# The odd layer's output projection between the attention's units, and four modulation runs elsewhere, in a two-model block kernel

## The reference, cut to what matters

```
cond = silu(c)
mod = cond @ ada_w[l] + ada_b[l]                 # 1024 -> 6 * 1024, both layers
sh1, sc1, g1, sh2, sc2, g2 = split(mod, 6)
h = rms_norm(x, norm_mix[l]) * (1 + sc1) + sh1
q, k, v = split(h @ w_in_odd)                    # 16 heads of 64, 4 key heads
q, k = rms_norm per head
y = banded attention with a sink per head, window 128, softmax over two blocks of 128 keys
x = x + g1 * (y @ w_out[l])
h = rms_norm(x, norm_ffn[l]) * (1 + sc2) + sh2
x = x + g2 * ((silu(h @ gate) * (h @ up)) @ down)
```

## Time and profile before

| | |
|---|---|
| median of three runs | 1477.8 us |
| the profiled execution: its time, its span | 1480.7 us, 1478.7 us |
| mean granted TensorE clock | 0.864 of full |
| PE busy | 1207.3 us, 82% |
| DVE busy | 615.7 us, 42% |
| ACT busy | 476.1 us, 32% |
| chain that ended last | PE 61%, DMA 21%, DVE 9%, ACT 5% |
| 16 DMA engines, main queue | 64.7% of the span |

### The profile page before, as it was taken

The page is one execution under the profiler, slowest core; times in us unless marked ns, Lnnn a source line. Parts: engine busy times, 40 slices in busy tenths (PEclk is TensorE's granted clock), DMA queues, the critical chain, the costliest instruction groups (busy, mean ns, idle before and its releaser), DMA issues.

```text
span 1478.7 us, 19441 instructions
## 1 busy us (share of the span) xinstructions
PE 1207.3 (82%) x7691; PEld 883.7 (60%) x7691; DVE 615.7 (42%) x1239; ACT 476.1 (32%) x769; POOL 7.6 (1%) x54
## 2 busy tenths in 40 slices
PE   5878886775676756847897888999999978999998
PEld 4655464442333323413675337899898734999986
DVE  3472643110010000101753576655535756565553
ACT  4561530100000000002532335554433447465441
POOL 1000000000000000000000000000000000000000
PEclk9897788888888877977897668899999988999999
DMA  8442347999999999999536431865536462665520
GB/s 292 172 152 76 115 173 320 428 430 429 430 430 428 430 430 428 430 425 403 197 129 228 171 114 58 253 207 201 195 145 226 171 253 90 203 196 174 203 109 29
DMA packets 121728, 368.67 MB, mean 249 GB/s; under 512 B 9842, under 2 KB 56093, under 8 KB 110878
## 3 DMA queue, kind: packets, MB, share of 16 engines
q1 hardware_dynamic: 120556, 367.26, 64.7%
q10 hardware_dynamic: 1074, 0.08, 0.1%
HBM read 366.28 MB, written 1.05 MB: 248 GB/s over the span
## 4 chain that ended last, share of the span: by engine, by line
PE 61%; DMA 21%; DVE 9%; ACT 5%; issue 3%; SPq 1%; DVEq 0%; ACTq 0%
PE ps L1810 58%; DMA more<-in_w_down_dram 7%; DMA more<-in_w_gate_dram 7%; DMA more<-in_w_up_dram 6%; PE ps L1814 3%; DVE st L32 2%; DVE ring_r L32 2%; DVE R_c L32 1%; SPq L664 1%; DVE R_a L32 1%; DVE X_c L32 1%; ACT X_c L32 1%; DVE sc L32 1%; ACT R_a L32 1%; ACT hn L32 1%
## 5 line engine op out<-in xcount | busy, mean ns | idle before, releaser
L1810 PE MATMUL ps<-hT_r,ring_r 128*128 128x256 f32 x864 | 245.5, 284 | 0.0
L1810 PE MATMUL ps<-ring,xg 128*32 128x512 f32 x640 | 140.4, 725 | 121.5 <-DMA more<-in_w_gate_dram 42.6
L1810 PEld LDWEIGHTS ps<-hT_r,ring_r 128*128 128x128 f32 x864 | 167.8, 194 | 0.0
L1810 PEld LDWEIGHTS ps<-ring,xg 128*32 128x32 f32 x640 | 35.2, 131 | 217.2 <-issue 217.2
L32 DVE TENSOR_TENSOR ring_r<-ring,W_c_r 128x1024 fp32r<-128x1024 f32 x94 | 115.2, 1226 | 97.5 <-ACT W_c_r L32 94.1
L1810 PE MATMUL ps<-R_c_r,W_c_r 128*128 128x256 f32 x608 | 153.1, 284 | 0.0
L32 DVE TENSOR_TENSOR ring_r<-ring,X_c_r 128x1024 fp32r<-128x1024 f32 x88 | 107.8, 1225 | 98.4 <-ACT X_c_r L32 95.7
L1810 PE MATMUL ps<-R_c_r,X_c_r 128*128 128x256 f32 x576 | 148.2, 285 | 0.0
L32 ACT ACTIVATE W_c_r<-ring 128x1024 fp32r<-128x1024 f32 x94 | 99.7, 1060 | 89.2 <-PE ps L1810 84.5
L32 ACT ACTIVATE X_c_r<-ring 128x1024 fp32r<-128x1024 f32 x88 | 93.3, 1061 | 90.3 <-PE ps L1810 85.4
L1810 PE MATMUL ps<-hT_r,W_c_r 128*128 128x256 f32 x416 | 119.0, 286 | 1.9 <-DVE R_c_r L32 1.8
(11 more groups left out here) (281 smaller groups left out, 1874.5 us busy)
## 6 DMA issues: line engine op xcount, KB each, us to landing
ring<-in_ada_w_dram SPq DMA_DIRECT2D x24, 2048.0 KB, 8.2
ring<-in_w_gate_dram SPq DMA_DIRECT2D x20, 2048.0 KB, 15.9
ring<-in_w_up_dram SPq DMA_DIRECT2D x20, 2048.0 KB, 20.7
ring<-in_w_down_dram SPq DMA_DIRECT2D x20, 2048.0 KB, 16.4
more<-in_w_up_dram SPq DMA_DIRECT2D x12, 2048.0 KB, 24.4
more<-in_w_gate_dram SPq DMA_DIRECT2D x12, 2048.0 KB, 23.1
more<-in_w_down_dram SPq DMA_DIRECT2D x12, 2048.0 KB, 23.6
ring<-in_ffn_gate_dram SPq DMA_DIRECT2D x22, 1024.0 KB, 5.6
```

Of the source, the lines that this page charges most:

```text
L1810: return pe.matmul(out, lhsT, rhs, start=start, stop=stop, skip_group_check=True)
```

## The change

The odd layer's attention and its output projection become one loop, `beside`. `pipeline` is split into a generator `ticks` and `run`, so that one tick can be taken at a time. In tick t = 4 + 2c every engine feeds chunk c of w_out, and PE uses it four ticks later, at t = 8, 10, ..., 18 for chunks 0 to 5; chunks 6 and 7 follow together after the last tick. PE waits for `s_fin` of unit 2c + 1 before chunk c.

To make room in PSUM the scores use banks 0 and 1 for every unit, the turned weights bank 2, and the projection sums banks 3, 4, 5 and 7. All eight chunks of w_out use three of the six high-part buffers (`narrow`).

The seven runs in the attention become three, at units 1, 3 and 5. Run 17 goes to q1's first chunk, run 18 to q1's fourth, runs 22 and 23 to chunks 6 and 12 of the odd layer's down product. The two loads of w_out move in SP's order from after run 21's to after run 19's.

```diff
+def beside(g, units, feed, i0, lag):
+    for t in range(units + 5):
+        next(g, None)
+        k = t - lag + 3
+        if t == lag - 1:
+            feed.side.end()
+        if k >= 0 and k % 2 == 0 and k < 16:
+            feed(i0 + k // 2)
+        elif k == 16:
+            feed.one()
+    feed.drain()
...
     p.product("q0", 4)
-    p.product("q1", 4)
-    p.units(4, 16, (0, 2, 4, 6, 8, 10, 12), 8, 2)
-    p.close(("o", 2))
+    p.ada(("f", len(p.chunks)))
+    k = p.load("w", "q1")
+    p.first["q1"] = len(p.chunks)
+    for q in range(4):
+        if q == 2:
+            p.close(("f", len(p.chunks)))
+        if q == 3:
+            p.ada(("f", len(p.chunks)))
+        p.feed(k, q)
+    p.units(4, 16, (1, 3, 5), 1, 2)
     p.out_proj(2)
-    p.ffn(1, False, None)
+    p.ffn(1, False, (6, 12))
...
-        beside = {first["wo", j] + c for j in range(3) for c in range(2)}
+        narrow = {first["wo", j] + c for j in range(3) for c in range(8 if j == 2 else 2)}
...
+        banks = [(0, 0, 1, 1, 2, 2, 3, 4), (0, 0, 1, 1, 2, 2, 3, 4), (3, 3, 4, 4, 5, 5, 7, 7)]
...
+        t4.score, t4.turned = lambda U, m: m, lambda U: 2
...
                 def used(i):
                     c = i - first["wo", j]
                     if c == 0:
-                        take(0, 1, 2, 3, 4)
+                        take(*(set(banks[j and 2 * j - 2]) if j else range(4)))
+                    if j == 2:
+                        pe.wait_ge(s_fin, t4.fin[2 * c + 1])
...
-            attend(4, 1, {0: [(s_hv, 19), (s_ev, 24), (s_lam, 1)], 8: [(s_hv, 21)]})
-            ada(("o", 2))
-            pe.wait_ge(s_fin, t4.end)
-            out_proj(2, hL_at, XFc, 0)
+            beside(attend(4, 1, {0: [(s_hv, 19), (s_ev, 24), (s_lam, 1)], 8: [(s_hv, 21)]}), 16,
+                   out_proj(2, hL_at, XFc, 0), first["wo", 2], 7)
```

More of the change, by code:

```diff
@@ L118, in pipeline, with run @@
                 stage(t - lag)
+        yield
+def run(g):
+    for _ in g:
+        pass
+def pipeline(n, *stages):
+    run(ticks(n, *stages))
+def beside(g, units, feed, i0, lag):
[9 more added lines that the diff above has]
+    feed.drain()
 class Plan:
@@ L171, in units, with ffn @@
                 self.out_loads(j)
-    def ffn(self, l, turn_run, run):
+    def ffn(self, l, turn_run, runs):
         self.first["gu", l] = len(self.chunks)
@@ L184, in ffn @@
             for q in range(min(4, 22 - 4 * u)):
-                if run is not None and 4 * u + q == run:
+                if 4 * u + q in runs:
                     self.ada(("f", len(self.chunks)))
-                if run is not None and 4 * u + q == run + 3:
+                if 4 * u + q - 3 in runs:
                     self.close(("f", len(self.chunks)))
@@ L881, in fins @@
                         copy(hH[:, unit.dst, unit.out], ps[6][:, unit.out], up=s_oh)
-                pipeline(len(at_n.units), (4, copies), (5, fins), (1, weights), (0, scores), (4, ahead))
+                return ticks(len(at_n.units), (4, copies), (5, fins), (1, weights), (0, scores), (4, ahead))
             def out_proj(j, tb, XF, attended):
@@ L990, in scalar @@
             side.add(work_gla())
-            attend(1, 1, [first["wo", 0], first["wo", 0] + 1], XF)
+            run(attend(1, 1, [first["wo", 0], first["wo", 0] + 1], XF))
             side.end()
@@ L1088, in scalar @@
             side.until(ev, "qk")
-            attend(2, 2)
+            run(attend(2, 2))
             def work_sub():
@@ L1096, in scalar @@
             side.until(ev, "sel0", "bT")
-            attend(3, 2, [first["wo", 1], first["wo", 1] + 1], XFc)
+            run(attend(3, 2, [first["wo", 1], first["wo", 1] + 1], XFc))
             side.end()
@@ L1157, in scalar @@
             side.until(ev, "qk0")
-            attend(4, 1, [first["wo", 2], first["wo", 2] + 1], XFc)
-            ada(("o", 2))
-            out_proj(2, 0, XFc, t4.end)
+            beside(attend(4, 1), 16, Feed(lambda i: begin(i, XFc), side), first["wo", 2], 7)
+            act.wait_ge(s_fin, t4.end)
             ffn(1, 3, 20)
@@ L1302, in fins @@
                           up=s_fin)
-                pipeline(len(at_n.units), (1, weights), (2, norms), (5, fins), (0, scores), (4, ahead))
+                return ticks(len(at_n.units), (1, weights), (2, norms), (5, fins), (0, scores), (4, ahead))
             def out_proj(j, gain, hL, XF):
@@ L1923, in features @@
                     for f in range(8):
-                        free[bank[f]] = C.next(s_xd)
+                        free[banks[n_][f]] = C.next(s_xd)
             def modulated(n, before, after=lambda: None):
@@ L1961, in out_proj @@
                 feed = Feed(begin, side, used)
+                if j == 2:
+                    return feed
                 for c in range(8):
@@ L2022, in values @@
                         free[6] = (s_fin, at_n.fin[u])
-                pipeline(len(at_n.units), (3, turns), (0, scores), (4, values))
+                return ticks(len(at_n.units), (3, turns), (0, scores), (4, values))
             pe.wait_ge(s_ident, 1)
@@ L2429, in used @@
                         if j == 0:
-                            take(0, 1, 2, 3, 4)
+                            take(*(range(4) if l else set(banks[1])))
                         if j % 2 == 0:
```

46 lines of the change are left out of this document (22 added, 24 removed).

## The result

The changed kernel took 1506.7 us, the median of four executions (1505.95 to 1508.22). The kernel before took 1479.55 us in four executions, the three shown above and one more. The ratio is 1.0181, with a 95% interval of 1.0156 to 1.0206: slower by 27 us, where I had forecast 6.7 us and a range that ended at 1492. The profiled execution took 1508.22 us with a span of 1506.2, at a mean granted clock of 0.868.

A forecast was written before the change was run, and what follows sets the result against it. PE was taken to bound the kernel nearly throughout from 1050 us on, except for holes in the attention. 10.2 - 14.5 + 3.1 + 7.9 = +6.7 us on the median of 1477.8 gave 1484.5 us, range 1475 to 1492.

The forecast's parts named there:

- Attention and projection: -14.5: From q1's end to the projection's last matmul: 14.5 us shorter, bounds -21 to -10.
- The first ticks: Attention's start: scores 8 begin 39.4 us after q1's end (before 35.4); the shared banks cost 6.8 us.
- The clock falls: Rival, chance 0.15: 1.2 GHz after stage q's stand and in ticks 4 to 7 adds 7 us, 1491.5.
- The steady pair: Attention ticks 8 to 15: a pair of units with a projection chunk takes 5.9 us, bounds 5.8 and 6.4.
- The end: Tick 16 on, without scores: last values and projection chunks 4 to 7, from 1246.7 to 1262.1 in trace time.
- One pair of banks costs nothing: Rival, chance 0.20: first eight attention ticks 6.8 us earlier, pairs 0.5 less, 1477.2 us, not slower.
- Stage q: +10.2: Stage q: two runs and two closes add 5.7 us, PE waits of 3.0 and 1.5 the rest; bounds 5.7 and 13.
- After it: +3.1: Behind the projection: DVE's additions to x end 5.3 us after PE's last matmul instead of 2.2; bounds 0 and 4.
- Feed-forward: +7.9: Odd layer's down product: two modulation runs and their closes in a PE stream without holes add 7.9 us.

The follow-up runs named there:

- run 17: Not a follow-up kernel: a modulation run on PE, moved by the change from the attention to q1's first chunk; took 3.64 us instead of 1.86.
- run 18: Not a follow-up kernel: a modulation run on PE, moved by the change from the attention to q1's fourth chunk; PE waited 1.65 us before it.
- Run 7: Changed kernel with 20 unread matmuls on PE, 10 in stage q's hole and 10 before unit 1's scores: 1500.5 us, ratio 1.0154.
- run 4: Changed kernel with scores of units 1, 3, 5 in banks 3 and 4, turned weights of units 1 and 3 in bank 5: 1499.2 us.
- run 3: Changed kernel with DVE making the low part of w_out's chunks 0 to 5 one tick later, behind that tick's maxima: 1500.65 us, ratio 1.0149.
- run 13: Changed kernel with run 17 moved from q1's first chunk to q1's second, loads in the same order: 1501.55 us, ratio 1.0149.
- Run 5: Changed kernel with PE's chunk of the projection ahead of the values of its tick: 1502.7 us, ratio 1.0178.
- run 6: Changed kernel with both the low part one tick later and PE's projection chunk ahead of the values: 1497.7 us, ratio 1.0134.
- Run 11: Changed kernel with no stage q runs, second score banks, later low parts, projection chunks before values, and x's additions before two gate low parts: 1480.6 us.
- run 1: Kernel before with only the change's modulation moves and earlier w_out loads; attention, banks and projection as before: 1494.3 us, ratio 1.0101.
- run 9: Changed kernel with a modulation close moved from q1's first chunk to q0's second: 1510.4 us, ratio 1.0192.

## Why the prediction was wrong

**The failed step is the term "Attention and projection: -14.5".** It came to +0.8, and all three parts of it were too short.

*The first ticks* were to reach scores 8 at 39.4 and did at 46.1 (+6.7). I had followed the three queues tick by tick, but with PE's durations of the fast clock from scores 2 on, and kept the clock as a rival with a chance of 0.15. My reason against it, that at half clock PE fills its own holes, is what happened before, where a second pair of banks let it run ahead. With one pair it can't: the waits for DVE's maxima (1.11) and ACT's copy (1.22) remain at 1.2 GHz, and the clock stays down. Run 7, which changes no wait, takes out 5.2 us; run 4, which undoes the shared banks, 9.0 with the clock that they cost; run 3, which only frees the maxima of ticks 4 and 6 from the chunks' low parts, 5.2; and run 13, with the same first ticks at a clock of 0.74 instead of 0.64, 3.3. These overlap and can't be added up. They also say that part of the 6.7 hangs on which stretches happen to run at 1.2 GHz.

*The steady pair* was to be 5.9 and was 7.0 to 7.1 (+3.7 over three pairs). I compared totals, 5.78 of PE, 6.1 of DVE, 5.4 of ACT, and took a little more than the larger. A total bounds a loop only if no engine waits in its own queue for another. Runs 3, 5 and 6 show two loops of 6.8 and 6.7 us, and that the pair falls to 6.1 or 6.2 only when both are cut. It falls no further, because the total of PE was too small as well: I had 2.95 for the attention's part and 2.83 for the chunk, and in run 6, with PE full at clock 1.00, they are 6.20 together. So of the 1.2 us a pair, 0.3 is PE's work and 0.9 the loops, with what the low clock until 1246 adds in the first pair. (The 2.83 has a slip of its own: 24 times the 0.119 in front of it is 2.86.)

*The end*, from scores 14 to the last projection matmul, was to be 21.3 and was 26.1 (+4.8), with 3.9 us of PE's waits for R_c_r in it. Run 5 alone brings it to 22.6, both edits to 22.0.

**The rivals.** "One pair of banks costs nothing" was decided at scores 8 before 33 us, and is refuted. "The clock falls" was right in its mechanism and its place, and priced at 7; run 7 measured 4 to 6. But it was put as an alternative to the forecast, and came on top of it. I had weighed the Trainium skill's page "TensorE: Matmul & The Clock Gate" here. Its section "A second HAM failure mode: psum-queue depth-cycling" says that a kernel whose matmul groups cycle through PSUM banks idles PE in small pieces often enough for the clock to go up and down. This trace agrees: 0.64, 0.50 and 0.78 for 36 us, and from 1209 to the fall at 1240 no single hole was longer than 1.32 us. Its report of a kernel to which a second set of PSUM buffers gave almost nothing (section "HAM oscillation — how this bites in real kernels") does not carry over: run 4 is such a second set for three units, and gave 7 us.

**Stage q: +10.2 forecast, +12.9 measured.** Both waits were there, with the releasers named: 5.87 before run 17, 1.65 before run 18, and run 18's transfer landed after about 8. What lacked was the clock behind the first (3.64 - 1.86 = 1.8 of the run, and kvo's chunk), which I had as a bound of 13. That the first wait was 3.0 in the forecast and 5.87 here cost little, since PE's head start made most of it.

**After it: +3.1 forecast, +5.1 measured.** 2.7 of it are the 32 sums, 6.30 instead of 3.63 at clock 0.58, which I had not counted; the other 2.4 are DVE's order, priced at 3.1. Run 11 undoes that order, and 4.2 us go, 1.6 of them in the sums: their low clock came with the wait. **Feed-forward: +7.9 forecast, +8.3 measured**, and 194.7 in every kernel with these two runs. Right.

In all: 15.3 + 2.7 + 2.0 + 0.4, and 0.4 ahead of the odd layer, are 20.8 us more than forecast, and before's median over four executions is 1.7 above the three I had started from. 1484.5 + 22.5 is 1507.0, against 1506.7. (The parts of the first term, 6.7, 3.7 and 4.8, make 15.2, the 15.3 but for rounding.)

Still open: what the gate chunks' first parts would give if they were begun in the last ticks, while the attention's weights hold these buffers. This wasn't tried. Nor is it separated how much of run 4's 9.0 us is waiting at full clock and how much the clock itself. Why kvo's first chunks get 0.50 in one execution and 1.00 in another is open too.

## What to carry to other kernels

Work that fills the holes of a stage paced by other engines does not pay back its full time when it is taken out, and taking it out can do harm twice: the holes open, and the clock falls for what follows. Moving four runs out of such places cost 15 us here (run 1). Price a hole at its length and at the longer operations behind it (a run of 1.86 us took 3.64).

When work is put between the stages of a pipeline, don't bound the loop by each engine's total: write the order of each queue down and follow one item around it, with the helper operations (here a chunk's high and low part) that stand ahead of the critical one. If one order is cut and the pair hardly moves, look for the second loop just beneath before giving the first up.

Where the plan puts a step on a queue that runs chunks ahead, count from where it stands on that engine, for a wait there holds back all the chunks in between: one chunk's place was 5 to 6 us of stage q in run 13, and a close put too early stood 9 us in run 9.

A hole read from one trace is as long as its engine was early in that execution. The hole before run 17 was 3.1 or 5.9 us, by the clock of the chunks ahead of it, and stage q took 60.2 to 61.1 with either. Take the time at which a wait ends, and not its length, into the sum.

## What the runs showed of the hardware that I had not expected

Useless matmuls can pay. 17 of them in the holes of the kernel before made it 3.1 us faster (0.9979, interval 0.9965 to 0.9993), and 20 in the changed one brought scores 8 forward by 5.2 us; the granted clock in these stretches went from 0.67 to 0.90, from 0.53 to 0.99, and from about 0.64 to 0.82. And a PE that is 80% busy in the profile can be one that is held back: from 1204 to 1228 it worked at a mean clock of 0.57. The same first ticks, with the same waits, took 46.1 or 42.8 us, at 0.64 and 0.74: one trace of such a stretch can be off by 3 us.
